# Splitting the attention heads' half of an output projection into three f32r products in a hybrid decoder layer

## Chip, cores and metric

The kernel runs on one core of a Trainium2 chip. The metric is the device time of one launch in microseconds (us). TensorE multiplies, ScalarE (ACT in the profile) and VectorE (DVE) work on the elements, GpSimd (POOL) and SyncE (SP) issue DMAs. The engines run their own instruction lists in order and wait for each other by semaphores.

## The reference, cut to what matters

One layer for 1024 prompt rows and 8 decode rows, all in float32, D_MODEL 1024:

```python
z = rmsnorm(x, g_mix) @ w_in                       # q, k, v, u of 512 columns each
attn = stick_breaking(q, k, v, ...)                # 8 heads x 64, strictly causal
pool = pool_mix(u, ...)                            # 4 groups x 128
mixed = concatenate([attn, pool], -1)              # 512 of the heads + 512 pooled
h = h + mixed @ w_out                              # the step that is changed
h = h + hier_moe(rmsnorm(h, g_ffn), ...)           # routing, 32 experts, top 2
gate = sigmoid(rmsnorm(h, g_ple) @ w_ple_gate)
h = h + gate * (p @ w_ple_proj)
```

In stick-breaking attention a weight is a sigmoid times the product of (1 - sigmoid) over the later keys, so each block needs two sigmoids, a scan along the keys and a product.

## The kernel before

The 1032 rows are 9 row tiles: tile 0 holds the 8 decode rows, tiles 1 to 8 have 128 prompt rows each. There are five stages. Stage 1 (0 to 286 us) multiplies by w_in, does the decode rows' attention and the pooling, and loads w_out into `w_out` (128 partitions, 8 blocks of 1024; blocks 0 to 3 hold the pooled rows of w_out, blocks 4 to 7 the heads' rows). Stage 2 (286 to 580 us) is the prompt's attention with the output projection woven in. Stage 3 (to 610 us) is the routing; it overlaps the first weight loads of the experts. Stage 4 runs the experts, stage 5 the last gate.

**Stage 2, units.** An attention unit is one row tile t, one pair of heads and up to four key blocks. Tiles 1 to 4 have 4 units each, tiles 5 to 8 have 8, 48 in all. For each unit TensorE does a "turn" (transposes the finished weights `beta` into `p_at`, line 987), the "scores" of the unit three ahead (line 974), and the "values" (line 997, into `p_o`). ScalarE takes the sigmoids (lines 1108, 1109) and copies `p_at` to `aT` (line 1116). VectorE scans and multiplies (lines 1191, 1196).

**Stage 2, pieces.** The projection of row tile j is done during the units of tile j+1 ("job" j). Its pieces are: k=1 heads' rows for columns 0 to 511, k=2 pooled rows for the same columns, k=3 and k=4 the same for columns 512 to 1023, k=5 ("rows") the transposes of the result, k=6 the router's logits. In a tile of 4 units they go (1,2), (3,4), (5), (6); in a tile of 8 units to units 0 to 6 with unit 4 empty. Job 8 is the tail behind the last unit, with the order pooled, values, pooled, heads, heads. VectorE adds the residual after k=2 and k=4 (`h`, line 1210) and multiplies by g_ffn (line 1212). At the end of a tile ScalarE copies the heads' output `p_o` to `mixT` ("attn", line 1122), which the heads' pieces read. A matmul with two f32 operands appears as two records.

**Order.** `plan`, `act_plan` and `dve_plan` are lists of such steps, built in one loop over the units; each engine walks its own. VectorE's list has the step "attn", and does nothing for it.

**f32r splitting.** Elsewhere (w_in, the experts, w_ple_proj) an f32 operand is split on ScalarE into hi (rounded to f32r) and on VectorE into lo = raw - hi, and the product is hi x hi + hi x lo + lo x hi, each a matmul of one pass.

**End of stage 2 and stage 3.** SyncE's list (`att_sp`): g_ffn, w_ple_proj, the routing constants at 286 us; then `pT_raw`; then the weights of the first two experts, six loads of 2 MB (`load_part`); then the 1/rms columns of the experts' input rows, and the stores of p times w_ple_proj. ScalarE splits `pT_raw` and `wp_raw` in piece (8,1) of the tail, VectorE makes the lo parts there, ahead of the additions of job 8. Later ScalarE copies the products of the last stage to `y` (`pp_copy`, line 1160), which from the third on wait for the store two before, splits the first expert's gate weights (line 1172), and TensorE transposes the first expert's gathered rows (line 2038).

## Time and profile before

| | |
|---|---|
| Median of 3 timed runs | 1335.0 us (1329.85 to 1335.48) |
| The profiled execution | 1331.11 us, its span 1329.3 us |
| TensorE matmul busy | 1283.1 us (97%), 6686 instructions |
| TensorE weight load busy | 940.9 us (71%) |
| VectorE busy | 869.1 us (65%) |
| ScalarE busy | 781.8 us (59%) |
| GpSimd busy | 201.2 us (15%) |
| HBM read, written | 308.55 MB, 38.16 MB; 261 GB/s over the span |
| Granted TensorE clock, mean | 0.985 of full speed |

The profile is one execution. Busy time counts a matmul from its start to the end of its result; since matmuls overlap, the distance between two starts is what one costs. A row of the timeline has the start, the duration, the engine, the line, the operation, "out<-in", the shape and how many were merged; in square brackets, how long the engine sat idle before and what ended that. A row of a group has the busy time and the mean duration in ns after the bar.

### The profile page before, as it was taken

The numbers are of one execution on the slowest core, as the hardware profiler recorded it, in microseconds if no ns is written. First come the engines' busy times: TensorE is split into PE (matmuls) and PEld (weight loads), VectorE is DVE, ScalarE is ACT, GpSimd is POOL, SyncE is SP. The second block draws the span as 40 slices with busy tenths as digits, with TensorE's granted clock in tenths as the row PEclk, the third lists the DMA queues.
The fourth block names the chain that finished last, engine by engine and source line by source line (L and its number), as shares of the span: only waits on it lengthen the run. The fifth ranks groups of instructions, "written<-read, shape, count | busy, mean of one in ns | idle before, by whom it ended". The sixth has DMA issues, their size and how long they took to land. (4 is left out here: it accounts for less than half of the span.)

```text
span 1329.3 us, 18289 instructions
## 1 busy us (share of the span) xinstructions
PE 1283.1 (97%) x6686; PEld 940.9 (71%) x6686; DVE 869.1 (65%) x792; ACT 781.8 (59%) x893; POOL 201.2 (15%) x207
## 2 busy tenths in 40 slices
PE   7999999999999999997999999999999999998998
PEld 3777666765565566656877778877788777875786
DVE  5445411124545667566888888889888888878554
ACT  5434411123455577536877877877877777776543
POOL 2100100000000000001222333222332223210000
PEclk9999999988999999999999999999999999998999
DMA  7867667361111111196899999999999999973651
GB/s 260 331 215 247 231 206 230 127 230 48 48 49 48 49 49 48 40 423 241 332 366 371 372 395 380 372 376 370 382 385 366 367 366 367 383 268 119 237 188 65
DMA packets 63292, 330.59 MB, mean 249 GB/s; under 512 B 12479, under 2 KB 12767, under 8 KB 49262
## 3 DMA queue, kind: packets, MB, share of 16 engines
q1 hardware_dynamic: 44798, 279.19, 54.3%
q0 software_dynamic: 18432, 50.56, 10.4%
q8 instruction: 39, 0.64, 0.2%
q14 instruction: 23, 0.19, 0.0%
HBM read 308.55 MB, written 38.16 MB: 261 GB/s over the span
## 5 line engine op out<-in xcount | busy, mean ns | idle before, releaser
L1396 DVE TENSOR_TENSOR w_lo<-w_gate,w_hi 128x2048 fp32r<-128x2048 f32 x64 | 146.6, 2293 | 40.2 <-ACT w_hi L1392 32.8
L1396 DVE TENSOR_TENSOR w_lo<-w_down,w_hi 128x2048 fp32r<-128x2048 f32 x64 | 146.4, 2287 | 12.4 <-ACT w_hi L1392 12.4
L1191 DVE TENSOR_TENSOR_SCAN keep<-keep 128x512 f32<-128x512 f32 (+3 forms) x96 | 88.6, 964 | 88.0 <-ACT beta L1109 88.0
L1396 DVE TENSOR_TENSOR w_lo<-w_up,w_hi 128x2048 fp32r<-128x2048 f32 x64 | 143.6, 2284 | 0.0
L1392 ACT ACTIVATE w_hi<-w_down 128x2048 fp32r<-128x2048 f32 x64 | 122.6, 1915 | 0.0
L1392 ACT ACTIVATE w_hi<-w_up 128x2048 fp32r<-128x2048 f32 x64 | 122.3, 1913 | 0.0
L1392 ACT ACTIVATE w_hi<-w_gate 128x2048 fp32r<-128x2048 f32 x62 | 118.6, 1914 | 0.0
L1407 PE MATMUL p_y<-w_hi,hiddenT_hi 128*128 128x512 f32 x256 | 104.2, 407 | 2.1 <-DVE hiddenT_lo L2201 2.1
L425 PE MATMUL p_z<-w_in_hi,xT_hi 128*128 128x512 f32 x256 | 105.4, 412 | 0.0
L1116 ACT ACTIVATE aT<-p_at 128x1024 f32<-128x1024 f32 (+3 forms) x48 | 39.5, 824 | 109.7 <-PE p_at L987 109.7
L1407 PE MATMUL p_u<-w_hi,xeT_hi 128*128 128x512 f32 x256 | 102.9, 402 | 0.0
L1407 PE MATMUL p_g<-w_hi,xeT_hi 128*128 128x512 f32 x252 | 101.4, 403 | 0.0
L1408 PE MATMUL p_y<-w_hi,hiddenT_lo 128*128 128x512 f32 x256 | 101.0, 394 | 0.0
L427 PE MATMUL p_z<-w_in_hi,xT_lo 128*128 128x512 f32 x256 | 100.6, 393 | 0.0
L426 PE MATMUL p_z<-w_in_lo,xT_hi 128*128 128x512 f32 x256 | 100.5, 392 | 0.0
L1408 PE MATMUL p_u<-w_hi,xeT_lo 128*128 128x512 f32 x256 | 100.1, 391 | 0.0
L1408 PE MATMUL p_g<-w_hi,xeT_lo 128*128 128x512 f32 x252 | 98.7, 391 | 0.0
L2018 POOL DMA_INDIRECT expert_rows<-y,idx_y x32 | 82.7, 2584 | 42.6 <-POOL idx_y L2013 27.5
L1413 PE MATMUL p_y<-w_lo,hiddenT_hi 128*128 128x512 f32 x256 | 69.8, 395 | 0.0
L1413 PE MATMUL p_u<-w_lo,xeT_hi 128*128 128x512 f32 x256 | 68.9, 391 | 0.0
L1413 PE MATMUL p_g<-w_lo,xeT_hi 128*128 128x512 f32 x252 | 68.3, 393 | 0.1
L425 PEld LDWEIGHTS p_z<-w_in_hi,xT_hi 128*128 128x128 f32 x256 | 48.5, 189 | 25.1 <-issue 16.3
(311 smaller groups left out, 2525.6 us busy)
## 6 DMA issues: line engine op xcount, KB each, us to landing
w_gate<-in_w_experts SPq DMA_DIRECT2D x32, 2048.0 KB, 13.1
w_up<-in_w_experts SPq DMA_DIRECT2D x32, 2048.0 KB, 16.3
w_down<-in_w_experts SPq DMA_DIRECT2D x32, 2048.0 KB, 8.3
v_sb<-in_cache_kT SPq DMA_DIRECT2D x64, 256.0 KB, 6.0
w_in_raw<-in_cache_v SPq DMA_DIRECT2D x64, 256.0 KB, 4.1
xT_raw<-in_xT_all POOLq DMA_DIRECT2D x16, 512.0 KB, 4.6
y_loaded<-expert_rows SPq DMA_DIRECT2D x8, 1024.0 KB, 6.9
x_res<-in_x_all POOLq DMA_DIRECT2D x9, 512.0 KB, 5.4
```

Of the source, the lines that this page charges most:

```text
L425: pe.matmul(z, x_hi[par][:, k, r], w_hi[:, k, cs], start=(k == 0), stop=False)
L426: pe.matmul(z, x_hi[par][:, k, r], w_lo[:, k, cs], start=False, stop=False)
L427: ins = pe.matmul(z, x_lo[par][:, k, r], w_hi[:, k, cs], start=False, stop=(k == KD - 1))
L1116: act.activation(aT[arg % 2][:].rearrange("p a b n -> p a (b n)")[:, :, 0:w], p_at[:].rearrange("p (a n) -> p a n", a=2)[:, :, 0:w], ACT.C ...
L1191: ins = dve.tensor_tensor_scan(out=row, data0=row, data1=row, initial=first, op0=ALU.mult, op1=ALU.bypass)
L1392: act.activation(w_hi[slot][:], chunk_of(c, par), ACT.Copy).then_inc(hi_ready, 1)
L1396: dve.tensor_tensor(out=w_lo[slot][:], in0=chunk_of(c, par), in1=w_hi[slot][:], op=ALU.subtract).then_inc(lo_ready, 1)
L1407: pe.matmul(out, a_hi[:, k0 + k, :], w_hi[slot][:, k, :], start=(first and k == 0), stop=False)
L1408: pe.matmul(out, a_lo[:, k0 + k, :], w_hi[slot][:, k, :], start=False, stop=False)
L1413: ins = pe.matmul(out, a_hi[:, k0 + k, :], w_lo[slot][:, k, :], start=False, stop=(last and k == KC - 1))
L2018: pool.indirect_dma_start(out=y_dram, out_offset=bass.IndirectOffsetOnAxis(ap=idx_y[par][:, 0:1], axis=0), in_=y_sb[par][:], in_offset=Non ...
```

## The change

The heads' half of the projection is done in three f32r products. The 4 heads' blocks of w_out are split once into `wo_hi` and `wo_lo`, in two halves of 512 columns, by a new step "split" behind the scores of units 0 and 1 on ScalarE and VectorE. `wo_lo` is written over the blocks it is made from. The heads' rows of each tile are copied to one buffer `mix_raw`, then to `mix_hi` on ScalarE, and `mix_lo` is made on VectorE; there is one set of buffers in place of two. Job 0's pieces move one unit later in tile 1, with pieces 5 and 6 in one unit. `w_out_hi` takes the place in which w_ple_proj was loaded and routing's scratch begins on the same place; `wp_raw` lies over the expert stage's `w_hi` now, which overlaps the attention's buffers, so its load moves from the start of the stage to behind the last unit's transposes. ScalarE waits for the lo part of w_ple_proj before it writes `w_hi`. The diff, cut to its core:

```diff
         p2 = ExitStack()
-        sb(p2, "w_out_place", [P, KD, D])
+
+        sb(p2, "w_out_pooled_place", [P, KD // 2, D])
+        wo_lo = sb(p2, "w_out_lo", [P, KD // 2, D], F32R)
...
-        mixT = [sb(p2, f"attn_mixed_T{i}", [P, AW // P, P]) for i in range(2)]
+        mix_raw = sb(p2, "attn_mixed_T", [P, AW // P, P])
+        mix_hi, mix_lo = (sb(p2, f"attn_mixed_T_{n}", [P, AW // P, P], F32R) for n in ("hi", "lo"))
         at_space = nc.sbuf_base
-        sb(p2, "space", [P, CHUNK])
...
+        wo_hi = sb(p2, "w_out_hi", [P, KD // 2, D], F32R)
+        at_consts = nc.sbuf_base
...
+        over_raw = ExitStack()
+        wp_raw = sb(over_raw, "w_ple_proj", [P, PLE // P, D])
+        over_raw.close()
         w_hi = [sb(moe, f"w_hi{i}", [P, KC, CHUNK], F32R) for i in range(2)]
...
-        over_raw = ExitStack()
-        wp_raw = sb(over_raw, "w_ple_proj", [P, PLE // P, D])
-        over_raw.close()
-        wp_lo = sb(p3, "w_ple_proj_lo", [P, PLE // P, D], F32R)
+
+        a_b = sb(p3, "assigned_bf16", [P, T9, E_ALL], BF16)
+        r8 = [sb(p3, f"r8_{i}", [P, T9, EPG]) for i in range(3)]
+        r32 = sb(p3, "group_experts", [P, T9, E_ALL])
...
+        sb(p3, "up_to_consts", [P, (at_consts - nc.sbuf_base) // 4])
...
-        tab = sb(p3, "slot_table", [P, 5, E_ALL])
+        wp_lo = sb(p3, "w_ple_proj_lo", [P, PLE // P, D], F32R)
...
+        wo_hi_ready, wo_lo_ready, mix_hi_ready, mix_lo_ready = whi_ready, wlo_ready, xhi_ready, xlo_ready
+        WO, MIX = 2 * KD, NP
...
                 return []
             per_job = len(of_tile) // len(mine)
             at = n - of_tile[0]
+            if units[n][0] == 1:
+                return [(0, k) for k in [(), (1, 2), (3, 4), (5, 6)][at]]
             return [(mine[at // per_job], k) for k in shares[per_job][at % per_job]]
...
-            act_plan += [("turn", n)] + rows + scores + dense + logit + end
-            dve_plan += logit + scores + dense + end
+            split = [("split", n)] if n < 2 else []
+            act_plan += [("turn", n)] + rows + scores + split + dense + logit + end
+            dve_plan += logit + scores + split + dense + end
...
         def att_sp(sp):
             sp.dma_start(g_ffn[:], A["g_ffn_bc"]).then_inc(s_c2, 16)
-            sp.dma_start(wp_raw[:].rearrange("p k n -> p (k n)"), A["w_ple_proj"]).then_inc(s_wp, 16)
             sp.dma_start(c3[:], A["c_route"]).then_inc(s_c3, 16)
             sp.dma_start(tri_f[:], A["c_tri"]).then_inc(s_c3, 16)
 
@@ -911,6 +922,9 @@
             sp.wait_ge(at_done, turns_to["rows", T_ALL - 2] + 1)
             sp.dma_start(pT_raw[:].rearrange("p k n -> p (k n)"), A["p_T0"]).then_inc(s_pt, 16)
 
+            sp.wait_ge(a_done, len(units))
+            sp.wait_ge(at_done, turns_to["turn", len(units) - 1] + 1)
+            sp.dma_start(wp_raw[:].rearrange("p k n -> p (k n)"), A["w_ple_proj"]).then_inc(s_wp, 16)
             sp.wait_ge(sc_done, len(units))
             load_part(sp, slice(0, 1), 0, w_g[0], s_wg[0])
             load_part(sp, slice(0, 1), 1, w_u[0], s_wu[0])
...
-                    if j == T_ALL - 1 and k < 5:
-                        n = (k - 1) // 2
-                        if k == 1:
-                            begin("h0")
-                        if k == 2:
-                            pe.wait_ge(attn_copied, T)
-                        pooled = k in (1, 3)
+                    def pooled_rows(n, first):
                         for kk in range(4):
-                            lhs = mixp[:, kk, T * P:(T + 1) * P] if pooled else mixT[T % 2][:, kk, :]
-                            ins = pe.matmul(bank(j, f"h{n}"), lhs, w_out[:, w_place(kk + (4 if pooled else 0)), n * CHUNK:(n + 1) * CHUNK],
-                                            start=(pooled and kk == 0), stop=(not pooled and kk == 3))
-                        if not pooled:
-                            ins.then_inc(w_done, 1)
-                        if k == 3:
-                            ins.then_inc(o_done, 1)
-                    elif k in (1, 2, 3, 4):
+                            ins = pe.matmul(bank(j, f"h{n}"), mixp[:, kk, T * P:(T + 1) * P], w_out[:, kk, n * CHUNK:(n + 1) * CHUNK],
+                                            start=(first and kk == 0), stop=(not first and kk == 3))
+                        return ins
+
+                    def head_rows(n, first):
+                        pe.wait_ge(wo_hi_ready, WO + n + 1)
+                        pe.wait_ge(wo_lo_ready, WO + n + 1)
+                        pe.wait_ge(mix_hi_ready, MIX + T + 1)
+                        out, cs = bank(j, f"h{n}"), slice(n * CHUNK, (n + 1) * CHUNK)
+                        for kk in range(4):
+                            pe.matmul(out, mix_hi[:, kk, :], wo_hi[:, kk, cs], start=(first and kk == 0), stop=False)
+                            pe.matmul(out, mix_hi[:, kk, :], wo_lo[:, kk, cs], start=False, stop=False)
+                        pe.wait_ge(mix_lo_ready, MIX + T + 1)
+                        for kk in range(4):
+                            ins = pe.matmul(out, mix_lo[:, kk, :], wo_hi[:, kk, cs], start=False, stop=(not first and kk == 3))
+                        return ins
+
+                    if k < 5:
                         n = (k - 1) // 2
                         if k == 1:
                             begin("h0")
                             pe.wait_ge(s_wout, 16 * KD)
-                            if T > 0:
-                                pe.wait_ge(attn_copied, T)
                         if k == 3:
                             begin("h1")
-                        for kk in range(4 * ((k - 1) % 2), 4 * ((k - 1) % 2) + 4):
-                            if kk < 4:
-                                lhs = (mixT[T % 2] if T > 0 else mixT_s)[:, kk, :]
-                            else:
-                                lhs = mixp[:, kk - 4, T * P:(T + 1) * P]
-                            ins = pe.matmul(bank(j, f"h{n}"), lhs, w_out[:, w_place(kk), n * CHUNK:(n + 1) * CHUNK], start=(kk == 0), stop=(kk == 7))
-                        if k in (2, 4):
+
+                        of_heads = (k % 2 == 1) != (j == T_ALL - 1)
+                        ins = (head_rows if of_heads else pooled_rows)(n, k % 2 == 1)
+                        if k % 2 == 0:
                             ins.then_inc(w_done, 1)
+                        if j == T_ALL - 1 and k == 3:
+                            ins.then_inc(o_done, 1)
                     if k == 6:
                         begin("logits")
                         pe.wait_ge(at_copied, turns_to["rows", j] + 1)
@@ -1117,9 +1132,17 @@
                                    p_at[:].rearrange("p (a n) -> p a n", a=2)[:, :, 0:w], ACT.Copy).then_inc(at_copied, 1)
                 elif what == "attn":
                     act.wait_ge(o_done, max(n for n in range(len(units)) if units[n][0] == arg) + 1)
-                    if arg >= 3:
-                        act.wait_ge(w_done, fills[jobs.index(arg - 2), "h1"] + 1)
-                    act.activation(mixT[arg % 2][:].rearrange("p c n -> p (c n)"), p_o[:], ACT.Copy).then_inc(attn_copied, 1)
+                    act.wait_ge(mix_lo_ready, MIX + arg)
+                    act.activation(mix_raw[:].rearrange("p c n -> p (c n)"), p_o[:], ACT.Copy).then_inc(attn_copied, 1)
+                    act.wait_ge(w_done, fills[jobs.index(arg - 1), "h1"] + 1)
+                    act.wait_ge(attn_copied, arg)
+                    act.activation(mix_hi[:], mix_raw[:], ACT.Copy).then_inc(mix_hi_ready, 1)
+                elif what == "split":
+                    cs = slice(arg * CHUNK, (arg + 1) * CHUNK)
+                    if arg == 0:
+                        act.activation(mix_hi[:], mixT_s[:], ACT.Copy).then_inc(mix_hi_ready, 1)
+                        act.wait_ge(s_wout, 16 * KD)
+                    act.activation(wo_hi[:, :, cs], w_out[:, KD // 2:, cs], ACT.Copy).then_inc(wo_hi_ready, 1)
...
             act.wait_ge(s_wg[0], 16)
+            act.wait_ge(p_lo, 2)
             for c in range(2):
                 act.activation(w_hi[c][:], w_g[0][:, KC * c:KC * c + KC, :], ACT.Copy).then_inc(hi_ready, 1)
...
+                elif what == "attn":
+                    dve.wait_ge(mix_hi_ready, MIX + arg + 1)
+                    dve.wait_ge(w_done, fills[jobs.index(arg - 1), "h1"] + 1)
+                    dve.tensor_tensor(out=mix_lo[:], in0=mix_raw[:], in1=mix_hi[:], op=ALU.subtract).then_inc(mix_lo_ready, 1)
+                elif what == "split":
+                    cs = slice(arg * CHUNK, (arg + 1) * CHUNK)
+                    if arg == 0:
+                        dve.wait_ge(mix_hi_ready, MIX + 1)
+                        dve.tensor_tensor(out=mix_lo[:], in0=mixT_s[:], in1=mix_hi[:], op=ALU.subtract).then_inc(mix_lo_ready, 1)
+                        dve.wait_ge(s_wout, 16 * KD)
+                    dve.wait_ge(wo_hi_ready, WO + arg + 1)
+                    dve.tensor_tensor(out=wo_lo[:, :, cs], in0=w_out[:, KD // 2:, cs], in1=wo_hi[:, :, cs],
+                                      op=ALU.subtract).then_inc(wo_lo_ready, 1)
```

## Rows read from the trace of the kernel before

**Rows 1.** Busy time by stretch; columns: us, each engine (instructions), clock, DMA share, GB/s

```profile
482.00:524.00 42.00, 41.22 (x299) 26.41 (x300) 28.72 (x30) 27.35 (x44) 1.58 (x3) 1.00 0.12 39
...
563.00:601.00 38.00, 32.10 (x208) 19.18 (x206) 24.75 (x64) 12.06 (x18) 2.93 (x4) 0.96 0.97 393
...
612.00:1100.00 488.00, 485.74 (x2239) 388.80 (x2240) 424.98 (x240) 374.68 (x294) 133.31 (x107) 1.00 0.91 367
```

**Rows 2.** Groups by line between 286 and 580 us: the heads' products

```profile
L1038 PE MATMUL p_w<-w_out_sb,attn_mixed_T 128*128 128x512 f32 x112 | 53.2, 619 | 0.6 <-DVE logits L1229 0.4
...
L1018 PE MATMUL p_sc<-w_out_sb,attn_mixed_T 128*128 128x512 f32 x16 | 7.0, 592 | 0.0
```

**Rows 3.** Timeline of TensorE, one heads' block in f32 (start, duration, first of what follows)

```profile
537.58 3.70 PE L1038 MATMUL p_w<-w_out_sb,attn_mixed_T 128*128 128x512 f32 x8
...
541.21 1.09 PE L997 MATMUL p_o<-aT,v_sb 128*64 128x128 f32 x16
```

**Rows 4.** Timeline of TensorE, f32r products of the same size in the first stage

```profile
211.15 0.39 PE L425 MATMUL p_z<-w_in_hi,xT_hi 128*128 128x512 f32 x1
...
212.29 0.39 PE L427 MATMUL p_z<-w_in_hi,xT_lo 128*128 128x512 f32 x1
...
212.60 1.06 PE L334 MATMUL p_b<-w_in_raw,decode_weights_T 128*32 128x512 f32 x8
```

**Rows 5.** Groups by line, page and stage: splits and copies of the added sizes

```profile
L1396 DVE TENSOR_TENSOR w_lo<-w_down,w_hi 128x2048 fp32r<-128x2048 f32 x64 | 146.4, 2287 | 12.4 <-ACT w_hi L1392 12.4
...
L1392 ACT ACTIVATE w_hi<-w_down 128x2048 fp32r<-128x2048 f32 x64 | 122.6, 1915 | 0.0
...
L1212 DVE TENSOR_TENSOR h_times_g<-h,g_ffn_sb 128x512 f32<-128x512 f32 x18 | 12.5, 692 | 0.6
...
L1122 ACT ACTIVATE attn_mixed_T<-p_o 128x512 f32<-128x512 f32 x8 | 5.0, 629 | 3.6 <-PE p_o L997 3.6
```

**Rows 6.** Timeline of the first tile's four units, 290 to 316 us

```profile
290.90 5.11 PE L1038 MATMUL p_w<-w_out_sb,attn_mixed_T_samples 128*128 128x512 f32 x8
...
291.91 0.38 ACT L1109 ACTIVATE beta<-p_sc,per_partition 128x128 f32<-128x128 f32 x1
...
307.89 0.44 PE L997 MATMUL p_o<-aT,v_sb 128*64 128x128 f32 x4
...
310.60 1.02 ACT L1137 ACTIVATE hT<-p_at 128x1024 f32<-128x1024 f32 x1 [1.42 <-PE p_at L1055]
...
315.04 0.70 PE L997 MATMUL p_o<-aT,v_sb 128*64 128x128 f32 x4
```

**Rows 7.** Busy time by stretch at the start of that tile (columns as in Rows 1)

```profile
290.00:294.00 4.00, 4.00 (x11) 2.12 (x11) 2.75 (x7) 1.95 (x8) 0.00 (x0) 0.52 0.99 393
```

**Rows 8.** Timeline of VectorE and TensorE at three changes of tile (3 to 4, 4 to 5, 7 to 8)

```profile
377.09 1.23 DVE L1196 TENSOR_TENSOR beta<-beta,keep 128x1024 f32<-128x1024 f32 x1
...
378.40 1.88 PE L1038 MATMUL p_w<-w_out_sb,pool_mixed_T 128*128 128x512 f32 x4
...
404.93 0.43 DVE L1196 TENSOR_TENSOR beta<-beta,keep 128x256 f32<-128x256 f32 x1
...
526.37 1.23 DVE L1196 TENSOR_TENSOR beta<-beta,keep 128x1024 f32<-128x1024 f32 x1
...
527.43 1.09 PE L997 MATMUL p_o<-aT,v_sb 128*64 128x128 f32 x16
```

**Rows 9.** DMA issues between 280 and 610 us: size, us from issue to landing

```profile
w_ple_proj<-in_w_ple_proj SPq DMA_DIRECT2D x1, 1024.0 KB, 7.3
...
expert_input_rows<-h_rstd_columns SPq DMA_DIRECT2D x1, 72.0 KB, 12.2
```

**Rows 10.** Timeline between 562 and 610 us: last loads' start and the experts' start

```profile
562.77 0.33 SPq L912 DMA_DIRECT2D pT_raw<-in_p_T  x1
...
600.27 1.02 ACT L1160 ACTIVATE y<-p_sc 128x1024 f32<-128x1024 f32 x1 [9.70 <-DMA p_times_w_ple_proj<-y]
...
609.72 1.09 PE L2038 MATMUL p_xe<-ident,x_gathered 128*128 128x128 f32 x8 [1.11 <-ACT y L1160]
```

26 lines of the change are left out of this document (12 added, 14 removed).

## The prediction, made before the changed kernel had run

> **What bounds the kernel now.** I read the busy time by stretch first, then the groups of the changed lines, then the timeline where the changed steps stand. In the attention stage TensorE is the bound: in the last full tile but one it is busy for 41.2 of 42 us, VectorE for 28.7, ScalarE for 27.4, and the DMAs for 12% [rows 1]. The expert stage is TensorE's as well, 485.7 of 488 us, so what delays its start moves the end by as much. Between the two lies a stretch with another bound: from 563 to 601 us the DMAs are busy for 97% and move 393 GB/s, while TensorE is at 32 of 38 us [rows 1]. The reader should see what ends that stretch. ScalarE's third copy to `y` starts at 600.27, after 9.7 us in which it waited for a store that was issued behind six weight loads; the 1/rms columns, 72 KB, took 12.2 us to land for the same reason [rows 9, 10]. From that copy a chain on ScalarE (two copies, the first expert's split, two copies) leads to TensorE's first transposes of the experts at 609.72, released by `y` [rows 10]. So a microsecond that TensorE saves before 563 us counts, one saved in the tail behind it does not, and a byte added to that stretch does.
>
> The Trainium skill says the same of the landing ("DMA: Bandwidth & Descriptors", "Queues, rings and completion order"): the semaphore increment lands only after every earlier write of that DMA engine. By that rule a load put in front of the weights delays each later store by its whole length; the 12.2 us for 72 KB agree [rows 9].
>
> **The products.** The heads' products are 112 records in tiles 2 to 8 and 16 in the tail [rows 2], and two blocks of 8 in tile 1 [rows 6]; 8 records are a block of four f32 products, so there are 14 + 2 + 2 = 18 blocks. A block took 3.63 us from its start to that of the values behind it (537.58 to 541.21) [rows 3]. f32r products of the same size stand 0.228 us apart (211.15 to 212.29 is five distances), and what follows the last comes 0.31 later; a block of 12 will take 11 x 0.228 + 0.31 = 2.8 us [rows 4]. That saves 0.8 us a block: 11.2 us in the 14 blocks of tiles 2 to 8, 1.6 in tile 1 (within its sum below), 1.6 in the tail. The tail's saving is put at nothing, for it lies in the DMA's stretch.
>
> The Trainium skill has 215.7 ns for a lone warm matmul of 512 columns ("TensorE: Matmul & The Clock Gate", "Back-to-back issue gap"). By it a block would take 2.6 us and the 14 blocks give some 3 us more; the trace's 0.228 us is for the same kind of product in a stream, and is used.
>
> **The new wait at a change of tile.** The heads' block k=1 of a job stands in the first unit of the next tile. Before, it waited for one copy of 0.63 us. Now it needs that copy, `mix_hi` behind it (about as long), and for its last four products `mix_lo`, 0.69 us on VectorE [rows 5]. Both come at the end of a tile in lists that run in order. On ScalarE `mix_hi` stands before the next `aT` copy, which the values need only behind the scores and the block: hidden. On VectorE the step stands behind the scan and product of the unit three ahead, and VectorE is late there, since the units at a tile's end have little dense work. At 7 to 8 that product ends at 526.37 + 1.23 = 527.60, `mix_lo` at 528.3, and with four products the values start at 529.3, against 527.43 before: 1.9 us later instead of 0.8 earlier, so the wait takes 2.7 [rows 8]. At 3 to 4: 378.32, 379.0, 379.9 against 378.40, 1.5 later, 2.3 for the wait [rows 8]. At 4 to 5 the product ends at 405.36, `mix_lo` would be there at 406.05, and the eight hi products last until then: no wait [rows 8]. Read in the same way, 1 to 2 has none, 2 to 3 has 1.5, 5 to 6 0.8, 6 to 7 1.5. Together 2.7 + 2.3 + 1.5 + 0.8 + 1.5 = 8.8 us. Behind `mix_lo` on VectorE is queued the scan that is needed three units later, so no one waits for that. The bounds are 0 (VectorE turns out early) and 8.8 plus a fall of the clock, below; I take 8.8, since it is read at the places themselves. At 8 to the tail VectorE has nothing queued and the pooled blocks cover it.
>
> Tiles 2 to 8: 8.8 - 11.2 = -2.4 us.
>
> **Tile 1.** The first heads' block now needs `wo_hi` and `wo_lo` of its half. ScalarE is through with the sigmoids at 292.3 [rows 6], then comes `mix_hi` 0.6, then 128x2048 in 1.92: 294.8. VectorE makes `wo_lo` in 2.29: 297.1 [rows 5]. TensorE has the first values, a turn and scores to do until 292.8, then stands for 4.4 us. Before, it began its block at 290.90 [rows 6]. After such a stop it starts at half clock (1.2 GHz), as it does in the stretch 290 to 294 with a granted clock of 0.52 [rows 7]. I give it 3 us of this, 6.6 products, and 5.4 at full clock: the block ends at 301.4, a pooled block and a pause of 0.5 bring the values of unit 1 to 305.3. The unit with k=3 and 4 took 8.5 us and takes 7.7: 313.0; in it the second half's split is covered, since `wo_lo` is there at about 301.5. In the last unit pieces 5 and 6 stand together. Before, from the values at 307.89 it was 2.7 us to the copy `hT` [rows 6]; so `hT` starts at 315.7 and ends at 316.8, and only then can the logits start, 2.2 us before the values: 319.0 against 315.04 [rows 6]. So tile 1 costs 4.0 us. It could be 2.5 (no half clock) or 6 (a second fall). What is queued behind the two splits (the copy `aT` of unit 1 and the sigmoids of unit 4 on ScalarE, their scan on VectorE) is needed only by steps behind the block that waits, so they delay nobody else.
>
> **The moved load.** `wp_raw`, 1.05 MB, was loaded at 286 us beside idle DMAs. Now it stands on SyncE's queue behind `pT_raw` (issued at 562.77 [rows 10]), with waits that are over by then, and ahead of all six weight loads, the 1/rms columns and the stores. Its length at the stretch's rate is 1.05 MB / 393 GB/s = 2.7 us [rows 1]. It can cost nothing if the DMAs have room after all, or 7.3 us if nothing overlaps it, its landing time in a quieter place [rows 9]; I take 2.7, as the share of 97% leaves no room. On the way it is needed too: it lands at about 570, ScalarE's hi takes 1.9 us and VectorE's lo 2.3, and the first addition of job 8 stands behind that at 574 in place of 573.4. With the shorter heads' blocks the later additions come no later than before, and what follows them waits for the stores' landing in any case: nothing, at most a microsecond. ScalarE's new wait for that lo part stands before `w_hi` behind the copies to `y`, long after it: nothing. Routing's scratch elsewhere: nothing, or below or above by tenths; no access pattern changes.
>
> **The sum.** 4.0 - 2.4 + 2.7 = +4.3 us. The profiled execution took 1331.1 us (its span and 1.8 around it), so it would be 1335.4; against the median of 1335.0, which lies 3.9 above it within a spread of 5.6, 1339.3. I give the latter.
>
> **Rivals.**
> *The waits vanish.* If VectorE is early at the changes of tile, the sum is 4.0 - 11.2 + 2.7 = -4.5: 1330.5. For it: only one order of small steps on VectorE decides, and TensorE's pace in the units before may differ by a microsecond. Against: five places are read, all alike. 12%. If the load is hidden as well and the tail's 1.6 us count, it is -8.8: 1326.2. Against it stands the 97%. 7%.
> *The clock falls at the new waits (slower).* A wait of 1 to 2 us with sparse transposes before it can bring TensorE to 1.2 GHz; the stretch 290 to 294, 4 us at 0.52, shows what this costs, 1.9 us a time [rows 7]. It decides from two falls on (+3.9, 1343.2); three give 1345. For it: the steps around a change of tile are short ones already. Against: with its present pauses a whole tile keeps a granted clock of 1.00 [rows 1]. 20%.
> *TensorE's saving is not the tile's.* If a unit is paced by sigmoid, scan and turn, the 14 blocks save nothing and each wait costs what it is late, 8.8 - 5 x 0.8 = 4.8: 4.0 + 4.8 + 2.7 = +11.5, 1346.5. Against: 41.2 of 42 us [rows 1]. With it I count that f32r products do not run at one pass here, against which stand [rows 4]. 9%.
>
> **How the numbers follow.** The forecast has 52%; by its own bounds (tile 1 from 2.5 to 6, waits a microsecond either way, the load from 1.5 to 4, the runs' spread) it holds from 1335 to 1344. This kernel's measurement can tell about 0.5%, 6.7 us, from no change: under 1328.3 is faster, over 1341.7 slower. Faster: the hidden load, 7%. Slower: 20 + 9% and a quarter of the forecast's, together 41%. Same: 52%. The range for 8 in 10 leaves out the hidden load and the last rival's upper half: 1330 to 1346.
>
> **What would show it.** Heads' blocks of 2.8 us without a wait; TensorE standing for about 4 us near 293 and pieces 5 and 6 touching a pause near 317; waits for `mix_lo` of 1 to 2 us in the first units of tiles 3, 4, 6, 7 and 8, none in 2 and 5; `pT_raw` issued about 1.6 us later; ScalarE's third copy to `y` about 4.3 us later, at 604.6, and the experts' first transposes by as much. It is wrong if the first waits are absent, if the granted clock is 0.5 in stretches of tiles 3 to 8, or if the time from `pT_raw` to the third copy stays at 37.5 us.

## The result, and the profile after

The changed kernel takes 1341.3 us (median of 12 runs, 1336.8 to 1343.0), the kernel before 1334.2 (12 runs, 1329.9 to 1338.0, the three of the table above among them). The ratio is 1.005, with a 95% interval from 1.0037 to 1.0064: slower by some 7 us. The forecast was +4.3 us and 1339.3. The change is thus 2.8 us above the forecast, the time only 2.0 us above it: the median of three runs that the forecast stood on was 0.8 us higher than that of the twelve. With twelve runs the interval is 0.14% to either side, finer than the 0.5% that the prediction had allowed for.

The profiled execution of after took 1341.4 us, its span is 1339.6 against 1329.3. I cut both spans at the same events: the first scores of the attention, the copy of the heads' output (`attn`) at the end of each tile, the issue of `pT_raw`, ScalarE's third copy to `y`, TensorE's first transposes of the experts (`p_xe`), and the end. "Tile 1" lasts from the first scores to its `attn` copy, "tile n" from one such copy to the next, and tile 8 to the issue of `pT_raw`.

| stretch | before | after | difference | forecast |
|---|---|---|---|---|
| start to first scores | 286.04 | 286.90 | +0.9 | 0 |
| tile 1 | 29.74 | 34.70 | +5.0 | +4.0 |
| tile 2 | 29.36 | 28.13 | -1.2 | -1.6 |
| tile 3 | 28.76 | 28.88 | +0.1 | -0.1 |
| tile 4 | 28.60 | 29.58 | +1.0 | +0.7 |
| tile 5 | 38.11 | 36.79 | -1.3 | -1.6 |
| tile 6 | 39.96 | 39.40 | -0.6 | -0.8 |
| tile 7 | 42.41 | 42.50 | +0.1 | -0.1 |
| tile 8 | 39.79 | 41.02 | +1.2 | +1.1 |
| `pT_raw` to third copy | 37.50 | 40.01 | +2.5 | +2.7 |
| third copy to `p_xe` | 9.45 | 10.39 | +0.9 | 0 |
| `p_xe` to the end | 719.58 | 721.30 | +1.7 | 0 |

Not every row of this table can be held against the forecast alike. Tiles 3 to 8 repeat to 0.1 us between profiles of the same instructions, but for two things named below (a fall of the clock, the issue of `pT_raw`). Tiles 1 and 2 don't: the kernel of the first experiment has the instructions of before in them and takes 30.89 and 26.38 us. The time to the first scores lies between 284.65 and 290.29 in the twelve profiles of this document, whose kernels are all alike up to there. And the profiled execution of before, 1331.1 us, is near its fast end, that of after is at its median, so the spans differ by more than the medians.

Line numbers of after are 11 to 37 higher than before's for the same statements (L1025 is the pooled product, L1035, L1036 and L1039 are the heads' three, L1225 makes `mix_lo`, L1233 `wo_lo`). The page of after:

```profile
span 1339.6 us, 18504 instructions
...
PE 1275.9 (95%) x6758; PEld 957.5 (71%) x6758; DVE 878.8 (66%) x803; ACT 791.2 (59%) x904; POOL 201.7 (15%) x207
```

TensorE is busy for 7 us less than the 1283.1 of before, and the span is 10 us longer: the arithmetic got cheaper, and TensorE stands longer. Where it stands, by the waits between 286 and 580 us of after (engine, tile and line that wait, what for: us in total, times, longest):

```profile
PE p_w L1039 <- DVE attn_mixed_T_lo L1225: 5.1, 5, 1.7
...
PE p_w L1035 <- DVE w_out_lo L1233: 3.4, 1, 3.4
...
PE p_w L1035 <- ACT attn_mixed_T_hi L1139: 1.8, 4, 0.6
PE p_w L1062 <- ACT hT L1160: 1.2, 1, 1.2
```

None of the four lines has a counterpart in before. The first tile, in the timeline of after (VectorE's split of the first half of w_out's blocks, then TensorE's first heads' block and the pooled one behind it; the last two rows are the logits and the values at the tile's end):

```profile
295.98 2.29 DVE L1233 TENSOR_TENSOR w_out_lo<-w_out_sb,w_out_hi 128x2048 fp32r<-128x2048 f32 x1 [0.58 <-ACT w_out_hi L1145]
...
298.53 0.76 PE L1035 MATMUL p_w<-w_out_hi,attn_mixed_T_hi 128*128 128x512 f32 x1 [3.42 <-DVE w_out_lo L1233]
299.09 0.63 PE L1036 MATMUL p_w<-w_out_lo,attn_mixed_T_hi 128*128 128x512 f32 x1
299.51 0.63 PE L1035 MATMUL p_w<-w_out_hi,attn_mixed_T_hi 128*128 128x512 f32 x1
...
303.69 3.60 PE L1025 MATMUL p_w<-w_out_sb,pool_mixed_T 128*128 128x512 f32 x8
...
318.91 2.02 PE L1062 MATMUL p_w<-w_router_sb,hT 128*128 128x36 f32 x16 [1.21 <-ACT hT L1160]
320.87 0.69 PE L1011 MATMUL p_o<-aT,v_sb 128*64 128x128 f32 x4
```

and the busy time by stretch there (us, each engine with its instructions, granted clock, DMA share, GB/s; to be held against [rows 7]):

```profile
294.00:298.00 4.00, 1.10 (x6) 0.19 (x4) 3.38 (x5) 4.00 (x8) 0.00 (x0) 0.50 0.00 0
298.00:302.00 4.00, 3.47 (x8) 2.81 (x9) 3.97 (x5) 1.40 (x1) 0.00 (x0) 0.50 0.00 0
302.00:306.00 4.00, 4.00 (x11) 2.40 (x10) 0.38 (x1) 0.00 (x0) 0.00 (x0) 0.80 0.00 0
```

TensorE stands for 3.4 us until `wo_lo` is there, and then works at half clock, 1.2 GHz, with 0.43 us from product to product, until about 303. It doesn't fall to half clock by that stop: the granted clock is 0.50 from the start of the stage on, in before too, where it rises at 293.8. After, then before, from where the clock falls to where it rises:

```profile
286.52:303.57 17.05, 12.82 (x50) 8.11 (x51) 11.89 (x21) 10.68 (x26) 1.04 (x2) 0.50 0.31 107
```

```profile
287.02:293.83 6.81, 6.11 (x24) 3.14 (x21) 4.65 (x12) 4.49 (x17) 0.47 (x1) 0.50 0.96 369
```

Waits at the changes of tile, timeline of after: the last four products of the first heads' block in tiles 4, 5 (no wait) and 8:

```profile
383.68 1.20 PE L1039 MATMUL p_w<-w_out_hi,attn_mixed_T_lo 128*128 128x512 f32 x4 [1.42 <-DVE attn_mixed_T_lo L1225]
...
411.98 1.09 PE L1039 MATMUL p_w<-w_out_hi,attn_mixed_T_lo 128*128 128x512 f32 x4
...
532.14 1.20 PE L1039 MATMUL p_w<-w_out_hi,attn_mixed_T_lo 128*128 128x512 f32 x4 [1.73 <-DVE attn_mixed_T_lo L1225]
```

These are the changes 3 to 4, 4 to 5 and 7 to 8 of the prediction. The end of the stage, against [rows 1, 9, 10]: the stretch's DMAs, the issue of `pT_raw`, the third copy, the first transposes, and the landing of the 72 KB:

```profile
568.00:608.00 40.00, 30.73 (x216) 21.23 (x214) 25.62 (x66) 12.39 (x20) 2.94 (x4) 0.91 0.98 399
```

```profile
567.90 0.33 SPq L923 DMA_DIRECT2D pT_raw<-in_p_T  x1
...
607.91 1.02 ACT L1183 ACTIVATE y<-p_sc 128x1024 f32<-128x1024 f32 x1 [14.44 <-DMA p_times_w_ple_proj<-y]
...
618.30 1.09 PE L2075 MATMUL p_xe<-ident,x_gathered 128*128 128x128 f32 x8 [1.11 <-ACT y L1183]
```

```profile
expert_input_rows<-h_rstd_columns SPq DMA_DIRECT2D x1, 72.0 KB, 15.5
```

### The profile page after: what moved, and what is told of

It reads as the page before. It is cut to its first block and busy times, and to the rows that moved or that the text cites. A ratio compares the mean times of both kernels' runs of the same rounds, so it can differ in the third digit from the quotient of the medians.

```text
span 1339.6 us, 18504 instructions
## 1 busy us (share of the span) xinstructions
PE 1275.9 (95%) x6758; PEld 957.5 (71%) x6758; DVE 878.8 (66%) x803; ACT 791.2 (59%) x904; POOL 201.7 (15%) x207
## 5 line engine op out<-in xcount | busy, mean ns | idle before, releaser
L425 PEld LDWEIGHTS p_z<-w_in_hi,xT_hi 128*128 128x128 f32 x256 | 48.1, 188 | 25.0 <-issue 16.3
## 6 DMA issues: line engine op xcount, KB each, us to landing
w_up<-in_w_experts SPq DMA_DIRECT2D x32, 2048.0 KB, 16.5
```

Source lines behind the costliest of these rows:

```text
L425: pe.matmul(z, x_hi[par][:, k, r], w_hi[:, k, cs], start=(k == 0), stop=False)
```

## The experiments

The theory was the sum of the prediction: (a) the 14 blocks save something each; (b) the waits for `mix_lo` eat most of it; (c) tile 1 pays for the splits, and partly in half clock; (d) the moved load pushes the DMA-bound stretch. The rivals: the order of the pieces, not the f32r products, is what counts; the load is hidden; the first tile's loss is the clock of the sparse work before it, whatever the wait; the stretch behind 563 us is bound by something else than bytes. The interval of a ratio to before is 2 to 3 us to either side, so two kernels whose medians differ by less than 4 us or so are told apart by their traces rather than by their times.

### The moved load alone, on the kernel before

```diff
 # att_sp, at the start of the stage
-sp.dma_start(wp_raw, ...)
 # att_sp, behind pT_raw
+sp.wait_ge(a_done, len(units))
+sp.wait_ge(at_done, turns_to["turn", len(units) - 1] + 1)
+sp.dma_start(wp_raw, ...)
 sp.wait_ge(sc_done, len(units))
```

> The kernel before, with one edit: the load of w_ple_proj moves from the start of the attention stage to behind pT_raw and ahead of the six weight loads, with the changed kernel's waits. Theory (the stretch is bound by the DMAs, and the load adds its length): from the issue of pT_raw to ScalarE's third copy to y 40.0 us instead of 37.5, the experts' first transposes later by 2.5 to 3.5 us, the attention tiles as before; ratio to before about 1.002. Rival (the load is hidden, and the changed kernel's loss behind 563 us comes from its tail): 37.5 us and no change, 1.000.

Measured: ratio to before 1.0021 (1.0007 to 1.0035), +2.8 us. Tiles 3 to 8 take 217.67 us (before 217.63), `pT_raw` to the third copy 40.00 in place of 37.50, and from there to `p_xe` 10.06 in place of 9.45. In its timeline:

```profile
564.85 0.33 SPq L911 DMA_DIRECT2D pT_raw<-in_p_T  x1
...
604.85 1.02 ACT L1162 ACTIVATE y<-p_sc 128x1024 f32<-128x1024 f32 x1 [13.77 <-DMA p_times_w_ple_proj<-y]
```

So (d) is shown: 2.5 us to the copy, the same as in after, and it isn't hidden.

The stretch behind the copy isn't the load's. What ends it is ScalarE's last copy to `y`, and that one waits for TensorE's last products for w_ple_proj (in before, the next to last and the last copy):

```profile
606.80 1.01 ACT L1160 ACTIVATE y<-p_sc 128x1024 f32<-128x1024 f32 x1
608.65 1.02 ACT L1160 ACTIVATE y<-p_sc 128x1024 f32<-128x1024 f32 x1 [0.83 <-PE p_sc L1067]
```

TensorE does 24 such products behind the third copy, and some of them at half clock, 0.43 us each in place of 0.23: 6 in the kernel with all pooled first and the late load (9.39 us to `p_xe`), 7 in before (9.45), 10 in this one and in the kernel with the early load again (10.06 both), 12 in after (10.39) and in the f32 kernel with the other order and the early load (10.41). The 0.9 us follow the clock in that stretch, and not the place of the load.

### The pooled rows first in tiles 2 to 8, on the changed kernel

```diff
-of_heads = (k % 2 == 1) != (j == T_ALL - 1)
+of_heads = (k % 2 == 1) != (j > 0)
```

Of each half of the columns the pooled block comes first now, which needs nothing of the last tile's end, and the heads' block behind it.

> The changed kernel, with the pooled rows first and the heads' rows second in jobs 1 to 7 (as job 8 has it); job 0, the load and all else stay. Theory (the seven blocks wait for the halves of the heads' rows, 6.9 us in all, and the saving of 11 us is real): all of these waits gone, tiles 2 to 8 shorter by 6 to 8 us than in the changed kernel, that is about 8 us shorter than before the change, and the whole about as fast as the kernel before (0.999 to 1.002). Rival (a unit is paced by sigmoid, scan and turn, so TensorE's saving reappears as waits for aT or the turn): the waits move to other lines and the ratio stays near 1.005.

Measured: 0.9988 of before (0.9972 to 1.0005). Tiles 3 to 8 take 210.27 us, against 218.17 in after and 217.63 in before: the waits for `attn_mixed_T_lo` and `attn_mixed_T_hi` are gone from the list, -7.9 us from after, and -7.36 from before. A whole heads' block, in its timeline at 526 us:

```profile
526.40 0.48 PE L1035 MATMUL p_w<-w_out_hi,attn_mixed_T_hi 128*128 128x512 f32 x1
526.71 0.39 PE L1036 MATMUL p_w<-w_out_lo,attn_mixed_T_hi 128*128 128x512 f32 x1
526.95 0.39 PE L1035 MATMUL p_w<-w_out_hi,attn_mixed_T_hi 128*128 128x512 f32 x1
...
528.36 1.09 PE L1039 MATMUL p_w<-w_out_hi,attn_mixed_T_lo 128*128 128x512 f32 x4
529.38 1.09 PE L1011 MATMUL p_o<-aT,v_sb 128*64 128x128 f32 x16
```

526.40 to 529.38 is 2.98 us, with 0.31 behind the first and the last product and 0.235 on average between, where I had put 2.8. Against the 3.63 of [rows 3] a block saves 0.65 us. Tiles 3 to 7 save 1.30 to 1.37 us each, two blocks, which is 0.65 to 0.69 a block. Tile 8 saves only 0.61, for it has a wait that neither before nor after has, in a later piece than the first:

```profile
533.34 2.84 PE L1025 MATMUL p_w<-w_out_sb,pool_mixed_T 128*128 128x512 f32 x6 [0.78 <-DVE h L1247]
```

With that 0.78 added back the 12 blocks save 8.1 us, 0.68 each. The new waits of after can now be read tile by tile, as what after takes more than this kernel:

| tile | after | this kernel | difference | forecast of the wait |
|---|---|---|---|---|
| 3 | 28.88 | 27.41 | 1.47 | 1.5 |
| 4 | 29.58 | 27.23 | 2.35 | 2.3 |
| 5 | 36.79 | 36.74 | 0.05 | 0 |
| 6 | 39.40 | 38.60 | 0.80 | 0.8 |
| 7 | 42.50 | 41.11 | 1.39 | 1.5 |
| 8 | 41.02 | 39.18 | 1.84, and 0.78 of this kernel's own wait: 2.62 | 2.7 |

That is 8.7 us in all, against 8.8. The list of waits shows 6.9 (5.1 and 1.8) for the same. A part of the difference is in how busy time is counted: a product lasts 0.39 us in the profile and the next could start after 0.235, so each of the nine waits looks some 0.16 us shorter than it is (an estimate, 1.4 us together). (a) and (b) are shown; (b) had the right size, (a) was too large by nearly a fifth.

The Trainium skill ("TensorE: Matmul & The Clock Gate", "Back-to-back issue gap") gives about 216 ns for the isolated gap of 512 columns and 131 ns for a sustained stream of weight loads and matmuls. By an estimate from the one a block would take 2.6 us, from the other 1.6; the 0.235 us here agrees with neither, and the row decides.

### The pooled rows first everywhere

```diff
-of_heads = (k % 2 == 1) != (j == T_ALL - 1)
+of_heads = k % 2 == 0
```

> The changed kernel, with the pooled rows first in every job, so in job 0 too. Theory: besides the seven waits, 3.4 us of pooled products at full length (more at half clock) cover most of the wait of 4 us for the first half's w_out_lo in tile 1, whose excess over before falls from 5.0 us to about 1 to 2; ratio to before 0.996 to 0.998. Rival (tile 1 is slow because of the clock and the pieces' later place, not because of the wait): tile 1 stays 4 to 5 us longer than before, and the run is like the one with jobs 1 to 7 alone.

Measured: 0.9968 (0.9949 to 0.9987). Tile 1 takes 29.3 us, 5.4 less than in after and 0.4 less than in before: in job 0 the pooled block stands where TensorE waited for `w_out_lo`, and no wait for it is left. Four profiles of kernels with these instructions in tile 1 have 29.3 to 30.9 us there (this one and three below), three with the f32 products 29.7 to 30.9. So most of the 5.0 us of tile 1 is a cost of the order in which the pieces stand, not of the splits as such. Tiles 3 to 8 take 211.42, 1.15 more than in the run before: here the granted clock is 0.50 from 395.4 to 398.9, at the change from tile 4 to 5, where no new wait stands.

### The same, and the load back at the start of the stage

```diff
+wp_raw = ...            # in the place of wp_lo, free during the attention
 # att_sp, behind g_ffn
+sp.dma_start(wp_raw, ...)
 # att_sp, behind pT_raw
-sp.wait_ge(a_done, len(units))
-sp.wait_ge(at_done, ...)
-sp.dma_start(wp_raw, ...)
```

> The changed kernel with the pooled rows first in every job, and w_ple_proj loaded at the start of the stage again, onto the place of its own lo part, which is made in place. Theory: 2.5 to 3.5 us less than the same without the early load, from pT_raw to the third copy to y 37.5 us again; ratio to before 0.993 to 0.996. Rival (the load costs nothing): the same as without it.

Measured: 0.993 (0.9915 to 0.9945), 1325.8 us, 3.5 below the last one and 8.4 below the kernel before. `pT_raw` to the third copy takes 37.43 us, as in before (37.50). By the interval that is 7 to 11 us below before, from five runs. This is the change nearly without its side costs: what the three f32r products give when nothing waits for them but the 0.78 us of tile 8.

### The order alone, on the kernel before

```diff
-for kk in range(8):
+for i8 in range(8):
+    kk = (i8 + 4) % 8
```

The products stay f32; only the halves change places.

> The kernel before (f32 products, early load), with the pooled rows first and the heads' rows second in jobs 0 to 7. Control for the order alone. Theory (the order only matters where halves are waited for; the kernel before waits for nothing there): tiles 3 to 8 take 217 to 218 us as before, ratio 0.999 to 1.001. Rival (part of what the order gave came from something else, such as the residual's addition ending earlier or the clock): a part of the 7 us shows up here, 0.996 or so.

Measured: 0.9995 (0.9976 to 1.0013), tiles 3 to 8 218.52 us against 217.63. The 0.9 us is only SyncE's later issue of `pT_raw`, the mark at which tile 8 is cut: from the `attn` copy of tile 7 to that of tile 8 it is 43.36 us against 43.35. The rival that the order is what counts falls: in f32, where the block waits only for one copy, the order is worth nothing.

### Job 0's pieces back to their old units

```diff
-[(), (1, 2), (3, 4), (5, 6)][at]
+[(1,), (2, 3, 4), (5,), (6,)][at]
```

On the kernel with all pooled first and the early load.

> The kernel with the pooled rows first and the early load, and job 0's pieces at (1), (2,3,4), (5), (6) of tile 1 in place of none, (1,2), (3,4), (5,6): the first pooled block fills unit 0, and rows and logits have units of their own again. Theory (what is left of tile 1's loss is TensorE idle before the first block and the 1.2 us for hT): tile 1 shorter by 1.5 to 3 us, ratio to before 0.991 to 0.993. Rival (tile 1 then waits for w_out_lo of the second half, or for the addition between h0 and h1 in one unit, as much as it gains): within 1 us of the same without it.

Measured: 0.9946 (0.9928 to 0.9965), 1329.2 us, 3.4 above its base, with intervals that overlap, so the tile has to tell it. I had expected tile 1 to be 1.5 to 3 us shorter; it takes 35.3 us in place of 30.9. The waits have moved, not gone, to the addition that the rival named:

```profile
307.63 5.40 PE L1023 MATMUL p_w<-w_out_sb,pool_mixed_T 128*128 128x512 f32 x8 [3.69 <-DVE h L1245]
```

The addition of h stands in VectorE's list behind the second split of w_out's blocks (304.69 to 306.98) and runs from 306.90; the next pooled block needs its bank. In the stretch behind, 306 to 314, the granted clock is 0.81 and 0.76. So with the pooled rows first the later place of job 0's pieces, which I had booked as a part of the loss, is the better one.

### Two products in place of three

```diff
-for kk in range(4):
-    pe.matmul(..., wo_hi[:, kk], mix_lo[:, kk], ...)
```

On the same base; the product of the heads' rows' lo part with w_out's hi part is left out, so this kernel doesn't compute the same sum.

> The kernel with the pooled rows first and the early load, with the third product left out (lo of the heads' rows times hi of w_out): 8 products of 12 in each of 18 blocks; the lo parts are still made. Theory (TensorE's time in a block is the tile's time, product for product): 4 x 0.235 = 0.94 us a block, 11.3 us in the 12 blocks of tiles 3 to 8, about 15 us in the 16 blocks before the tail, none from the tail's two. Rival (units are paced by ScalarE and VectorE once the blocks are short): less than 8 us in tiles 3 to 8, with new waits for h, for the turn or for aT.

Measured: 0.9851 (0.9827 to 0.9876), 1314.4 us, 11.4 below its base. Tiles 3 to 8 take 201.12 us, 9.1 less, where 12 blocks x 4 x 0.235 is 11.3. The rest is in VectorE's `h`: in tile 8 the base's wait of 0.78 us for it has grown to 1.71, and tile 7 has a new one of 0.75, together 1.7 us more:

```profile
516.93 3.70 PE L1023 MATMUL p_w<-w_out_sb,pool_mixed_T 128*128 128x512 f32 x8 [1.71 <-DVE h L1242]
```

So TensorE is the bound for about four fifths of a further saving in this stage; behind it VectorE is next.

### A heads' block that TensorE has something to do before

```diff
+if j == 0 and k == 1:
+    for kk in range(2):
+        pe.matmul(bank(j, "h0"), mixp[:, kk, T * P:(T + 1) * P], w_out[:, kk, 0:CHUNK], start=(kk == 0), stop=(kk == 1))
```

On the changed kernel; the two products are overwritten by the block's first one.

> The changed kernel, and in job 0, ahead of the first heads' block, two f32 products more (4 records) into the same bank, which the block's own first product then overwrites: TensorE has something to do while it waits for w_out_lo. Nothing of the computation is left out. Theory (part of the first tile's +5.0 us is that TensorE comes out of this wait at half clock, 0.50 until 302, so that the block at 298.53 takes 5.2 us, where a block at full clock took 2.98): the clock rises some 3 us earlier, the first block takes 2.8 to 3.3 us, first scores to the end of tile 1 go from 34.7 to 32.4 to 33.2 us, the median down by 1.5 to 2.5 us. Rival (the start of the block is set by w_out_lo, and the clock is lost by the whole of the sparse work before, not by this wait): the block still takes over 4.5 us, tile 1 stays at 34.7 within 0.3, the median within 0.7 us of the changed kernel's.

Measured: 1338.6 us, 1.0024 of before (1.0008 to 1.0039), 2.7 less than the changed kernel; the two intervals just overlap. Its timeline and its stretches:

```profile
296.57 3.48 PE L1052 MATMUL p_w<-w_out_sb,pool_mixed_T 128*128 128x512 f32 x4
300.04 0.47 PE L1035 MATMUL p_w<-w_out_hi,attn_mixed_T_hi 128*128 128x512 f32 x1
300.34 0.40 PE L1036 MATMUL p_w<-w_out_lo,attn_mixed_T_hi 128*128 128x512 f32 x1
...
302.86 3.59 PE L1025 MATMUL p_w<-w_out_sb,pool_mixed_T 128*128 128x512 f32 x8
```

```profile
298.00:302.00 4.00, 4.00 (x12) 2.01 (x11) 3.97 (x5) 3.07 (x5) 0.00 (x0) 0.79 0.00 0
302.00:306.00 4.00, 4.00 (x13) 2.02 (x11) 2.05 (x1) 0.00 (x0) 0.00 (x0) 1.00 0.01 4
```

The stage starts 2.0 us later in this profile (first scores at 288.92 in place of 286.90), so times count from there. The block takes 2.8 us in place of 5.2, tile 1 31.8 in place of 34.7. The block's start is still set by `w_out_lo`, which ends at 299.93 (297.64 + 2.29), 11.0 us behind the first scores (11.4 in after). The two f32 products run at half clock in the wait, and the clock is back at 299.7, 10.7 us behind the first scores in place of 16.7, so 6 us earlier:

```profile
289.44:299.66 10.22, 9.80 (x38) 4.62 (x37) 7.27 (x14) 9.19 (x25) 0.93 (x2) 0.50 0.52 176
```

That isn't the chance of one execution. The kernel with pooled first in tiles 2 to 8 has the wait too, and its clock is back 16.5 us behind the first scores; in the four kernels with all pooled first, job 0 in its new place and all three products, which have work there, it is 9.8 to 11.1 us. Work that is thrown away gains 2.9 us in the tile, a little more than the 1.5 to 2.3 that I had expected. So of the 5.0 us of tile 1 some 2.3 (the block) to 2.9 are half clock, and the rest is the wait and the later logits; the rival (the clock is lost whatever is done in the wait) falls.

### Weight loads behind the columns: one

```diff
 # att_sp
-load_part(sp, slice(1, 2), 2, w_d[1], s_wd[1])
 # in the loop of the stores of p times w_ple_proj, behind T == 1
+sp.wait_ge(w_done, fills[T_ALL - 1, "h1"] + 1)
+load_part(sp, slice(1, 2), 2, w_d[1], s_wd[1])
```

On the kernel with all pooled first and the early load: the second expert's w_down, 2 MB, is the last thing of these loads that anyone needs.

> The kernel with the pooled rows first and the early load, with the last of the six weight loads (w_down of the second expert, 2.1 MB) issued behind the 1/rms columns and the first two stores. Theory (the stretch's bytes set when the third copy to y and the gather start): 2.1 MB / 393 GB/s = 5.3 us less to the third copy, and 3 to 5 us less to the experts' first transposes, as routing's table is ready only about 3.5 us before the columns land now; the load is used 40 us later, so nothing is given back. Rival (the stretch is bound by routing, or the late load delays the first experts): less than 1.5 us.

Measured: 0.9891 (0.9867 to 0.9916), 1320.5 us, the lowest of the kernels that compute everything, 5.3 below its base and 13.7 below the kernel before. `pT_raw` to the third copy takes 32.5 in place of 37.4, and from there to `p_xe` 12.5 in place of 10.1, so the transposes come 2.5 us earlier. What the gather of the first expert's rows waits for has changed (POOL, base first, then this kernel), from a transfer to routing:

```profile
596.85 1.08 POOL L970 DMA_INDIRECT x_gathered<-expert_input_rows,m_row_of_slot  x1 [21.43 <-DMA expert_input_rows<-h_rstd_columns]
```

```profile
587.61 1.22 POOL L971 DMA_INDIRECT x_gathered<-expert_input_rows,m_row_of_slot  x1 [17.44 <-DVE m_row_of_slot L1347]
```

It starts 4.0 us earlier, counted from `pT_raw`. But the transposes aren't released by it; they stand behind the last copy to `y`, as before. The fifth and the sixth copy, and the transposes:

```profile
594.93 1.02 ACT L1182 ACTIVATE y<-p_sc 128x1024 f32<-128x1024 f32 x1 [2.85 <-DMA p_times_w_ple_proj<-y]
596.23 1.02 ACT L1182 ACTIVATE y<-p_sc 128x1024 f32<-128x1024 f32 x1 [0.27 <-DMA p_times_w_ple_proj<-y]
```

```profile
597.30 1.54 PE L2074 MATMUL p_xe<-ident,x_gathered 128*128 128x128 f32 x6 [5.52 <-ACT y L1182]
```

The fifth copy waits for the third store, which stands behind the moved load now. So half of what the transfers gave to the third copy went back to the fifth, and the transposes gain less than the 3 to 5 us expected. 2.5 us of the 5.3 by the medians stand in the stage; the rest isn't in these two profiles' stretches one by one (tiles 1 and 2 together are 3.3 us shorter, with the same instructions, see the last section), so I take 2.5 us for what is shown.

### Weight loads behind the columns: two

```diff
-load_part(sp, slice(1, 2), 1, w_u[1], s_wu[1])
 # behind T == 1, ahead of w_down
+load_part(sp, slice(1, 2), 1, w_u[1], s_wu[1])
```

> g4, and also w_up of the second expert is issued behind the last stage's columns and the first two stores. Nothing is left out. Theory (in g4 the bound has passed from the transfers to the routing: the gather starts at 587.61, released by VectorE's m_row_of_slot, no longer by a DMA): the third copy to y comes 4 to 5 us earlier again, but the first experts' transposes by less than 1 us, and the median is within 1 us of g4's 1320.5, or up to 2 us later if the second expert then waits for w_up. Rival (the transfers still set the transposes): 3 to 5 us more gained, median about 1316.

Measured: 0.9906 (0.9883 to 0.9928), 1322.9 us, 2.4 above the last one, which the medians alone don't tell from nothing; the profiled execution is one of the two longest of the six, 1328.1 us. The 72 KB land after 4.8 us in place of 9.1 and the third copy comes 30.1 us behind `pT_raw` in place of 32.5; yet the gather starts 35.9 behind it (35.3 with one load moved), and the transposes 48.1 in place of 45.0. The rival (3 to 5 us more gained) falls, and so does a part of my own expectation, for the transposes come 3 us later. I had taken routing for the next bound. The row that tells otherwise is the fifth copy to `y`:

```profile
600.14 1.02 ACT L1182 ACTIVATE y<-p_sc 128x1024 f32<-128x1024 f32 x1 [7.05 <-DMA p_times_w_ple_proj<-y]
...
603.59 1.97 PE L2074 MATMUL p_xe<-ident,x_gathered 128*128 128x128 f32 x8 [8.55 <-ACT y L1182]
```

It waits for the third store, which is queued behind both loads now, 4 MB; at 393 GB/s [rows 1] the second of them is 5.3 us. TensorE's transposes stand behind the last copy to `y`. Moving the loads past two stores pushes the wait from the third copy to the fifth, with one load already, and with two the loss there is larger than the gain.

## Why the prediction came out as it did, point by point

The sign, the place of every new wait and what each of them costs were as forecast; the kernel is 7 us slower by the medians against +4.3, with the products' saving put too high and tile 1's cost too low. The single steps:

- **The products: mis-sized.** Forecast 2.8 us a block and 0.8 saved; measured 2.98 in the block shown, and 0.68 saved over 12 blocks. The distance of 0.228 us came from a stream in the first stage [rows 4]; in that block it is 0.235, and the first product has 0.31 besides the last. 14 blocks save 9.5 us in place of 11.2. This is the largest error of the sum, 1.7 us too hopeful.
- **The waits at the changes of tile: right in place and size.** Five waits for `mix_lo` and none at 1 to 2 and 4 to 5, as forecast; 8.7 us by the second experiment against 8.8, and each of the five within some 0.1 us. The reading from VectorE's own position in [rows 8] holds. The five stretches of 4 us behind these waits have a granted clock of 1.00.
- **Tiles 2 to 8 together: -0.7 us measured, -2.4 forecast.** Tiles 3 to 8 are +0.5 against -0.8, and that is the products. Tile 2's -1.2 against -1.6 tells little, since the same instructions took 26.4 us there in another profile and 29.4 in before.
- **Tile 1: right in the wait, mis-sized in the clock.** Forecast +4.0, measured +5.0 (+3.8 against the first experiment's tile 1, the same instructions as before's). TensorE stood for 3.4 us; the 4.4 of the prediction is 4.3 by its own numbers. The block starts 11.6 us behind the first scores, forecast 11.1. It takes 5.2 us, forecast 4.3: I had given 3 us of it to half clock, and it was nearly the whole block (0.43 us from product to product to 302.07). The prediction had the half clock come from the stop; TensorE was at half clock from the start of the stage, 286.5, and stayed there to 303.6, while with work in the wait it rose 6 us earlier. What followed took 0.4 less than forecast. The filler puts the price of the clock at 2.3 to 2.9 us.
- **The moved load: right.** Forecast 2.7, measured 2.5, in after and alone.
- **From the third copy to the experts: taken as a chain on ScalarE, but +0.9.** The last of its two copies waited 0.83 us for TensorE's products even in before. The chain leads through TensorE, and its length goes with the number of products at half clock, 7 in before and 12 in after, in kernels with the early and the late load alike. By the runs it is no part of the load's price.
- **The rest.** `p_xe` to the end is +1.7 in these two profiles, and from 719.6 to 721.5 in the profiles of kernels that have the same instructions there; the start is +0.9, where twelve profiles spread over 5.6. Neither comes from the change as far as the runs show, and both are in the 10.3 us by which the spans differ.
- **The rivals.** "The waits vanish" was wrong at all five places. "The clock falls at the new waits" was wrong where it was put: none of the five waits cost any clock. There is a fall at the change 4 to 5 in three other profiles (the filler's, and two with all pooled first), and none of the five waits stands there. "TensorE's saving is not the tile's" is refuted by the second experiment, where the saving appears in full. The chance of "slower" adds up to 42%, not 41; nothing hangs on it. What would have shown me wrong (no waits, 0.5 in tiles 3 to 8, 37.5 us to the third copy) did not appear.
- **The signs to look for.** The third copy came 7.6 us later in the profile (600.27 to 607.91), forecast 4.3; `pT_raw` 5.1 later (562.77 to 567.90), forecast 1.6. The difference is 0.9 of the start, 1.0 of tile 1 and 1.7 of the tiles.

By what the runs show, the change's own sum is 5.0 - 0.7 + 2.5 = +6.8 us, beside +7.05 by the medians. That they meet so closely is partly luck: against the first experiment's tiles 1 and 2, which took 57.3 us where before took 59.1, the sum would be 1.8 higher. The gain that the change was worth was there all the time (9.5 us in the 14 blocks); waits for `mix_lo` and `mix_hi` took 8.7 of it, the wait for `wo_lo` with its half clock took 4 to 5, and the load 2.5. With the pooled rows first and the load early, the same products make the kernel faster by 8.4 us, and with one weight load moved by 13.7.

## What to carry to other kernels

When operands are split before a product, put the part of the sum that needs no split first: here one changed condition in the order of two halves turned +7 us into -4. Count the added steps on the engine that makes the operand at the point in its list where it stands, for there it can be late, however idle the engine is on average; read so, each of the waits came out within some 0.1 us. A stretch at 97% DMA makes every byte put in front of a small transfer count; move the bytes behind it, but look at what else then stands behind them.

## What was not expected of the hardware

- Two products of wasted work ahead of a wait made a tile 2.9 us shorter: TensorE was back at 2.4 GHz 10.7 us behind the first scores in place of 16.7 (16.5 in the other kernel with the wait).
- The clock's state in tiles 1 and 2 differs between executions of the same instructions: these two tiles take 58.3 us in the profile of the kernel with all pooled first and the early load, and 55.0 in that with one load moved, which has other instructions only from 560 us on. The first has a granted clock of 0.50 for 10.2 us in tile 1 and 6.8 in tile 2, the second for 10.2 in tile 1 alone. Some 3 us of any single profile of this kernel are chance for that reason; tiles 3 to 8 of the two agree better, 210.25 and 211.43, and there the difference is a fall of the clock too, at 395 us.
- In a stream of f32r products of 512 columns the distance is 0.235 us in this stage (the block shown) and 0.228 in the first, and 0.31 behind the first product of a block that follows other matmuls. Such small differences took 0.12 us a block off a saving that I had put at 0.8.
- 72 KB on a queue behind six loads of 2 MB took 12.2 us to land in before and 13.6 with all pooled first and the early load, 15.5 with the moved load ahead of them too, 9.1 behind five loads and 4.8 behind four.
